# A hybrid retention block on eight cores: the order of the casts in stage A and of the per-head projections

## The chip, the cores and the metric

The kernel runs on the 8 cores of one Trainium2 chip. Each core does the same program on its own two sequences of the batch of 16 (4096 tokens), without talking to the others. The time is device microseconds of the slowest core. Each core has TensorE (PE, with its weight loads PEld), VectorE (DVE), ScalarE (ACT), GpSimd (POOL, unused here) and SyncE (SP, which issues all DMAs of this kernel). Each takes its instructions in the order of its own list.

## The reference

One layer of a streaming encoder, width 1024, 4 retention heads with keys of 256 and values of 512. Cut to what matters here:

```python
h = layer_norm(x, ln0_g, ln0_b)
z = h @ w_in                       # conv (2x1024), q, k (1024), v, g (2048), two gates (1024)
cv, cg, q, k, v, g, ga, gb = split(z)
u = silu(layer_norm(causal_depthwise_conv(cv * sigmoid(cg), conv_w, conv_b)))
y_conv = u @ w_conv_o + b_conv_o
q = rotary(q, positions); k = rotary(k, positions) * dk ** -0.5
# per head, in chunks of 64: intra-chunk scores with decay, plus a carried state
y = ((q @ k.T) * decay) @ v + (q * xi) @ state
state = state * gamma_chunk + (k * zeta).T @ v
r = head_group_norm(y, ret_gn_g)
y_ret = (silu(g) * r) @ w_ret_o
mix = sigmoid(ga + b0) * y_conv + sigmoid(gb + b1) * y_ret
h = layer_norm(alpha * h + mix @ w_out)
# then a gated FFN of 2816 with a causal conv of width 3, a gated per-layer embedding, a last layer_norm
```

## The kernel before

A prologue turns all weights from float32 into bf16 copies in HBM, through FA, HT32 and HID. Then eight blocks of 512 tokens run one after the other (the loop over blk, L476), four for each sequence. A small scheduler (Sched, L46) keeps one list per engine in the order of the Python code; it adds semaphore waits from the records (Buf) that each operation reads and writes, and reorders nothing. So the order of the code is each engine's order of work. All compute instructions are recorded in helpers: matmuls L333, transposes L336, activations L344, tensor_tensor L347, scalar_tensor_tensor L356, copies and casts L359, DMA L362.

Stage A (L483 to L516) takes four tiles (tti) of 128 tokens: XS is loaded (two buffers; the first two tiles of a block are loaded during the block before), DVE takes statistics of XS (L490 to L492, into SMALL), ACT takes the square root, DVE reciprocal and a scalar op (L494, L495), ACT normalises XS in place, PE transposes it in eight pieces into two PSUM banks, ACT writes the eight pieces to HT32 (float32, L508), and DVE casts each to BB (bf16, L510). BB, also called HB, is the moving or stationary operand of all projections.

Then come the positions and the cosine and sine tables CS, the convolution branch, and stage C, the loop over four heads (L607 to L691). For each head h: q and k (16 matmuls of 512 columns each, then six DVE operations of rotary each over RT, into QT and KT_), v (64 matmuls of 256 columns; ACT copies to VV), g (64 more; ACT applies Silu into FC), transposes of KT_ into the bf16 bank PSB and ACT copies with a scale to KZ. Then the retention loop over four tiles of 128 tokens: scores (2 matmuls, one bank), SD = scores x mask on DVE, a product SD x VV and two QT x SBF (one bank, py), two KZ x VV (two banks), from which DVE updates the state SF and ACT its bf16 copy SBF; g1, g2 and g3 normalise py over its row (bn_stats on DVE, square root on ACT, reciprocal and scalar op on DVE, RN on ACT, the product with FC into RB_ on DVE), g2 one tile late and g3 two. At its end 16 transposes of RB_ through PSB and four ACT copies fill RTT. Then the next head begins. QT, KT_, KZ, VV, SD and RB_ have one buffer each, all cut from HID, which the convolution and the FFN also use. alias_barrier carries waits over from one use of HID to the next.

PSUM has seven float32 banks, handed out in a ring by next_ps (L321), and PSB. Weights come through wload (L446): chunks of 512 KB into a ring of four slots WR, issued by SP in the order of the code, each as soon as the matmuls of four chunks earlier are through with the slot.

Of the kernel before, what the change touches and what calls it, by code (L numbers as in the profile page):

```python
# [18 lines left out]
H = 4  # L19
# [241 lines left out]
def build_nc(nblk=NBLK, stop=None):  # L261
# [17 lines left out]
    with contextlib.ExitStack() as st:  # L279
# [33 lines left out]
        PT = sb("PT", [128, 2, TB], BF16)  # L313
        ZHT = sb("ZHT", [128, 176], F32)
# [73 lines left out]
        QT = HID[:, 0:1024].rearrange("p (d t) -> p d t", d=2)  # L388
        KT_ = HID[:, 1024:2048].rearrange("p (d t) -> p d t", d=2)
        KZ = HID[:, 2048:3072].rearrange("p (t d) -> p t d", t=4)  # L390
        VV = HID[:, 3072:5120].rearrange("p (t e) -> p t e", t=4)
        SD = HID[:, 5120:5632].rearrange("p (t i) -> p t i", t=4)
        RB_ = HID[:, 5632:7680].rearrange("p (t e) -> p t e", t=4)
        bQT, bKT, bKZ, bVV, bSD, bRB = Buf("qt"), Buf("kt"), Buf("kz"), Buf("vv"), Buf("sd"), Buf("rb")
        HIDV = HID[:, :].rearrange("p (j t) -> p j t", j=NJ)
        bHID = [Buf("hid%d" % j) for j in range(NJ)]
        hid_groups = {"u": bU, "head": [bQT, bKT, bKZ, bVV, bSD, bRB], "hid": bHID}
# [78 lines left out]
        for blk in range(nblk):  # L476
# [4 lines left out]
            if stop == 'pos':  # L481
                break
            for tti in range(4):  # L483
# [12 lines left out]
                act(XS[:, s, :], XS[:, s, :], AF.Identity, [bXS[s], bsm], [bXS[s]], bias=SMALL[:, c0 + 15:c0 + 16], scale=SMALL[:, c0 + 14:c0 + 15])  # L496
                if stop == 'A1':
                    continue
                for half in range(2):
                    pt_, bpt = next_ps()  # L500
                    for q in range(4):
                        f = half * 4 + q
                        tr(pt_[:, q * 128:(q + 1) * 128], XS[:, s, f * 128:(f + 1) * 128], IDF[:], [bXS[s], bID], [bpt])
                    if stop == 'A2':
                        continue
                    for q in range(4):
                        f = half * 4 + q
                        act(HT32[:, f, tti * 128:(tti + 1) * 128], pt_[:, q * 128:(q + 1) * 128], AF.Identity,  # L508
                            [bpt, bPAR], [bHT[f]], bias=pc("ln0_b", f), scale=pc("ln0_g", f))
                        cp(BB[:, f, tti * 128:(tti + 1) * 128], HT32[:, f, tti * 128:(tti + 1) * 128], [bHT[f]], [bBB[f]])  # L510
# [96 lines left out]
            for h in range(H):  # L607
# [14 lines left out]
                for part in range(2):  # L622
                    Ws = [wload("w_in", (16 if part == 0 else 24) + 2 * h + c2) for c2 in range(2)]
                    for tti in range(4):
                        pb, bpb = next_ps()
                        for c2 in range(2):
                            W, bW = Ws[c2]
                            for kt in range(8):
                                mm(pb[:, c2 * 256:(c2 + 1) * 256], HB[:, kt, tti * 128:(tti + 1) * 128], W[:, kt, :], kt == 0, kt == 7,
                                   [bW, bHB[kt]], [bpb])  # L630
                        if part == 0:
                            act(VV[:, tti, :], pb[:], AF.Copy, [bpb], [bVV])
                        else:
                            act(FC[:, tti, :], pb[:], AF.Silu, [bpb], [bFC[tti]])
# [4 lines left out]
                for tti in range(4):  # L639
                    act(KZ[:, tti, :], PSB[:, tti * 256:(tti + 1) * 256], AF.Copy, [bPSB, bPAR], [bKZ], scale=pc("zs", h))  # L640
                pys = {}

                def g1(tti):
                    c0 = 64 + tti * 16
                    bsm = bSMR[tti]
                    py, bpy = pys[tti]
                    S.op("dve", (lambda p_, c_: lambda e: e.bn_stats(out=SMALL[:, c_:c_ + 6], in_=p_[:]))(py, c0), [bpy], [bsm])  # L647
                    S.op("dve", (lambda c_: lambda e: e.bn_aggr(out=SMALL[:, c_ + 6:c_ + 8], in_=SMALL[:, c_:c_ + 6]))(c0), [bsm], [bsm])
                    act(SMALL[:, c0 + 8:c0 + 9], SMALL[:, c0 + 7:c0 + 8], AF.Sqrt, [bsm, bPAR], [bsm], bias=pc("epsx", h))

                def g2(tti):
                    c0 = 64 + tti * 16
                    bsm = bSMR[tti]
                    py, bpy = pys[tti]
                    rn = tti % 2
                    S.op("dve", (lambda c_: lambda e: e.reciprocal(out=SMALL[:, c_ + 8:c_ + 9], in_=SMALL[:, c_ + 8:c_ + 9]))(c0), [bsm], [bsm])
                    stt(SMALL[:, c0 + 9:c0 + 10], SMALL[:, c0 + 6:c0 + 7], -1.0, SMALL[:, c0 + 8:c0 + 9], ALU.mult, ALU.mult, [bsm], [bsm])
                    act(RN[:, rn, :], py[:], AF.Identity, [bpy, bsm], [bRN[rn]], bias=SMALL[:, c0 + 9:c0 + 10], scale=SMALL[:, c0 + 8:c0 + 9])
# [29 lines left out]
                for e4 in range(4):  # L688
                    for tti in range(4):
                        tr(PSB[:, tti * 128:(tti + 1) * 128], RB_[:, tti, e4 * 128:(e4 + 1) * 128], IDB[:], [bRB, bID], [bPSB])  # L690
                    act(RTT[:, h * 4 + e4, :], PSB[:, 0:512], AF.Copy, [bPSB], [bRTT[h * 4 + e4]])  # L691
            for mp in range(4):
# [174 lines left out]
```

How the kernel before makes its waits and increments, by code:

```python
                def body(eng):  # L139
                    for i, o in enumerate(self.ops[engname]):
                        for (key, val, kind) in o["waits"]:
                            if kind == "c":
                                eng.wait_ge(sems[key][val % NS], cum[key][val])
                            else:
                                eng.wait_ge(sems[key], val)
                        if o["fn"] is None:
                            continue
                        ins = o["fn"](eng)
                        if o["inc"] is not None:
                            ins.then_inc(sems[o["inc"][0]], o["inc"][1])
                        elif o["need"]:
                            ins.then_inc(sems[engname][i % NS], 1)
```

## Time and profile before

| | us |
|---|---|
| median of two runs | 6075.39 |
| the two runs | 6067.71, 6083.07 |
| the profiled execution | 6061.24 |
| its span (slowest core, core 5) | 6059.5 |
| spans of the eight cores | 6040.0 to 6059.5 |
| PE busy | 3906.8 (64%) |
| DVE busy | 2753.4 (45%) |
| ACT busy | 2093.0 (35%) |

The profile is of one execution on the slowest core. Busy times are sums over the span; matmuls are pipelined and their ends are modelled. A row of the timeline gives start, length, engine, line, operation, tiles and count, and in brackets how long the engine was idle before it and which engine, tile and line it then waited for. The granted clock of TensorE is given as a share of full speed (2.4 GHz); here its rows are at 0.50 (1.2 GHz), at 1.00, or at a mean between. Where an instruction waits for several semaphores, the wait is put down to the one that came last.

### The profile page before, as it was taken

The page shows a single profiled execution, that of the slowest core. Times are in us where ns is not written, and L with a number is a line of the kernel's source. Part 1 is how long each engine was busy: PE and PEld are TensorE (multiplying, and loading weights), DVE is VectorE, ACT ScalarE, POOL GpSimd, SP SyncE. Part 2 cuts the span into 40 slices and gives each one's busy share as a digit, 9 for nine tenths or more (in the row PEclk, how much of TensorE's full clock was granted, in tenths as well). Part 3 has the DMA queues.
Part 4 walks back from the last instruction along what each step waited for, and adds up shares of the span by engine and source line. Part 5 has one row for each costly group of instructions (what it writes and reads, how often), then busy time and mean ns, then how long its engine had stood idle before and what let it go on. Part 6 is the DMA issues. An engine that isn't in the chain of part 4 may idle for free.

```text
span 6059.5 us, 61462 instructions; the slowest of 8 cores (6040.0 to 6059.5 us)
## 1 busy us (share of the span) xinstructions
PE 3906.8 (64%) x18688; PEld 1883.6 (31%) x18688; DVE 2753.4 (45%) x4886; ACT 2093.0 (35%) x3448; POOL 0.2 (0%) x4
## 2 busy tenths in 40 slices
PE   0006677586775768667765867767675867757686
PEld 0002332233332333224322343233332333323332
DVE  1214437353464436453374435553374433644354
ACT  1113334323333333333343333333343333433333
POOL 0000000000000000000000000000000000000000
PEclk9999779797897879887787878978797877978798
DMA  9992223221232113212222112222132222321132
GB/s 317 330 321 77 70 73 100 81 68 59 84 108 79 56 56 111 80 58 84 84 85 98 59 57 94 91 72 70 63 107 74 69 69 77 104 83 53 60 107 85
DMA packets 162226, 586.57 MB, mean 97 GB/s; under 512 B 17648, under 2 KB 26480, under 8 KB 151408
## 3 DMA queue, kind: packets, MB, share of 16 engines
q1 hardware_dynamic: 161904, 582.64, 29.0%
q8 instruction: 158, 2.59, 0.2%
q14 instruction: 164, 1.34, 0.1%
HBM read 516.51 MB, written 66.06 MB: 96 GB/s over the span
## 4 chain that ended last, share of the span: by engine, by line
PE 47%; DVE 25%; DMA 9%; ACT 9%; issue 8%; DVEq 1%; SPq 0%; ACTq 0%
PE PS L333 45%; DVE FA L356 10%; DVE HID L347 3%; DVE HT L347 2%; DVE SF L356 2%; DMA WR<-w_ffn_down_bf 2%; ACT HT L344 2%; ACT HID L344 1%; DMA HT<-w_in 1%; DVE FA L347 1%; DVE SMALL L647 1%; ACT RN L344 1%; PE PSB L336 1%; DMA FA<-w_in 1%; ACT RTT L344 1%
## 5 line engine op out<-in xcount | busy, mean ns | idle before, releaser
L333 PE MATMUL PS<-BA,WR 128*128 128x512 bf16 x4352 | 1066.4, 391 | 376.7 <-DVE BA L359 137.4
L333 PE MATMUL PS<-BB,WR 128*128 128x512 bf16 x3072 | 786.9, 415 | 66.6 <-DMA WR<-w_in_bf 56.7
L333 PEld LDWEIGHTS PS<-BA,WR 128*128 128x128 bf16 x4352 | 416.0, 99 | 1005.2 <-issue 575.8
L356 DVE SCALAR_TENSOR_TENSOR FA<-PS,PAR,FA 128x511 f32<-128x511 f32 x704 | 525.5, 746 | 59.8 <-ACT FA L344 21.7
L336 PE MATMUL PS<-IDF,XS 128*128 128x128 f32 x256 | 62.1, 424 | 713.4 <-ACT XS L344 713.4
L344 ACT ACTIVATE FA<-PS,PAR 128x512 f32<-128x512 f32 x416 | 316.6, 761 | 512.5 <-PE PS L333 443.3
L333 PE MATMUL PS<-HID,DG 128*128 128x512 bf16 x1984 | 448.8, 390 | 43.5 <-DVE DG L574 43.5
L333 PEld LDWEIGHTS PS<-BB,WR 128*128 128x128 bf16 x3072 | 322.6, 106 | 491.5 <-issue 191.3
L333 PE MATMUL PS<-HID 128*128 128x512 bf16 (+1 forms) x640 | 224.9, 435 | 372.2 <-ACT RN L344 211.9
L333 PE MATMUL PS<-WR,BB 128*128 128x256 bf16 x4096 | 452.4, 273 | 0.0
L333 PEld LDWEIGHTS PS<-WR,BB 128*128 128x128 bf16 x4096 | 400.8, 98 | 53.2
L333 PE MATMUL PS<-HID,WR 128*128 128x512 bf16 x1408 | 340.1, 401 | 94.2 <-DMA WR<-w_ffn_down_bf 94.2
L574 DVE TENSOR_TENSOR DG<-IDB,PAR 128x3968 bf16<-128x3968 bf16 x64 | 273.9, 4290 | 139.5 <-PE PS L333 139.5
L356 DVE SCALAR_TENSOR_TENSOR SF<-SF,PS 128x512 f32<-128x512 f32 x256 | 164.6, 684 | 290.1 <-PE PS L333 290.0
L333 PEld LDWEIGHTS PS<-HID,DG 128*128 128x128 bf16 x1984 | 196.3, 99 | 296.1 <-issue 72.0
L347 DVE TENSOR_TENSOR RT<-PS,CS 128x512 f32<-128x512 f32 x256 | 168.0, 688 | 263.2 <-PE PS L333 252.9
L347 DVE TENSOR_TENSOR FC<-PS,FC 128x512 f32<-128x512 f32 x128 | 88.5, 692 | 435.3 <-PE PS L333 308.2
L344 ACT ACTIVATE SBF<-SF 128x512 bf16<-128x512 f32 x256 | 157.0, 629 | 357.7 <-DVE SF L356 356.6
L336 PEld LDWEIGHTS PS<-IDF,XS 128*128 128x128 f32 x256 | 50.2, 224 | 723.8 <-issue 723.8
L344 ACT ACTIVATE FC<-PS,PAR 128x512 f32<-128x512 f32 x192 | 131.0, 682 | 398.8 <-PE PS L333 398.6
L344 ACT ACTIVATE BB<-HT 128x512 bf16<-128x512 f32 x128 | 80.6, 629 | 537.6 <-DVE HT L347 460.1
L344 ACT ACT_TABLE_LOAD x145 | 186.0, 1283 | 221.5 <-DVE RT L356 75.4
(91 smaller groups left out, 4073.2 us busy)
## 6 DMA issues: line engine op xcount, KB each, us to landing
WR<-w_in_bf SPq DMA_DIRECT2D x320, 512.0 KB, 3.8
WR<-w_ffn_up_bf SPq DMA_DIRECT2D x176, 512.0 KB, 3.3
WR<-w_ffn_down_bf SPq DMA_DIRECT2D x128, 352.0 KB, 3.2
WR<-w_ret_o_bf SPq DMA_DIRECT2D x64, 512.0 KB, 3.9
FA<-w_in SPq DMA_DIRECT2D x20, 1024.0 KB, 12.2
HT<-w_in SPq DMA_DIRECT2D x20, 1024.0 KB, 12.0
w_in_bf<-HID SPq DMA_DIRECT2D x40, 512.0 KB, 9.1
XS<-x SPq DMA_DIRECT2D x32, 512.0 KB, 3.5
```

Of the source, the lines that this page charges most:

```text
L333: S.op("pe", lambda e: e.matmul(out, lhsT=lhsT, rhs=rhs, start=start, stop=stop), r, w)
L336: S.op("pe", lambda e: e.transpose(out, in_, ident), r, w)
L344: S.op("act", lambda e: e.activation(out=out, in_=in_, func=func, **kw), r, w)
L347: S.op("dve", lambda e: e.tensor_tensor(out=out, in0=in0, in1=in1, op=op), r, w)
L356: S.op("dve", lambda e: e.scalar_tensor_tensor(out=out, in0=in0, scalar=scalar, in1=in1, op0=op0, op1=op1), r, w)
L574: S.op("dve", (lambda g_, f_: lambda e: e.tensor_tensor(out=DG[:, g_, :, :], in0=IDB[:].unsqueeze(1).broadcast_to([128, 31, 128]), in1=PAR ...
L647: S.op("dve", (lambda p_, c_: lambda e: e.bn_stats(out=SMALL[:, c_:c_ + 6], in_=p_[:]))(py, c0), [bpy], [bsm])
```

## The change

Two edits.

Stage A: the eight casts of HT32 to BB are not recorded at once but collected, and recorded after the XS activation of the next tile; those of the fourth tile follow the loop.

Stage C: the body of the head loop is cut into three functions, proj_qkv (q, k, rotary, v), proj_g_kz (g, the transposes of k, KZ) and ret_loop (the rest, unchanged but for the buffers it reads). QT, KT_ and VV get two buffers each, chosen by h % 2; SD moves to a tensor of its own (1 KB per partition). The order becomes qkv(0), g_kz(0), qkv(1), ret(0), g_kz(1), qkv(2), ret(1), g_kz(2), qkv(3), ret(2), g_kz(3), ret(3). The order of the weight chunks on SP and of the PSUM banks follows it.

```diff
+        SDT = sb("SDT", [128, 4, 128], BF16)
...
-        QT = HID[:, 0:1024].rearrange("p (d t) -> p d t", d=2)
-        KT_ = HID[:, 1024:2048].rearrange("p (d t) -> p d t", d=2)
-        KZ = HID[:, 2048:3072].rearrange("p (t d) -> p t d", t=4)
-        VV = HID[:, 3072:5120].rearrange("p (t e) -> p t e", t=4)
-        SD = HID[:, 5120:5632].rearrange("p (t i) -> p t i", t=4)
-        RB_ = HID[:, 5632:7680].rearrange("p (t e) -> p t e", t=4)
-        bQT, bKT, bKZ, bVV, bSD, bRB = Buf("qt"), Buf("kt"), Buf("kz"), Buf("vv"), Buf("sd"), Buf("rb")
+        QTs = [HID[:, 1024 * i:1024 * (i + 1)].rearrange("p (d t) -> p d t", d=2) for i in range(2)]
+        KTs = [HID[:, 2048 + 1024 * i:2048 + 1024 * (i + 1)].rearrange("p (d t) -> p d t", d=2) for i in range(2)]
+        KZ = HID[:, 4096:5120].rearrange("p (t d) -> p t d", t=4)
+        VVs = [HID[:, 5120 + 2048 * i:5120 + 2048 * (i + 1)].rearrange("p (t e) -> p t e", t=4) for i in range(2)]
+        RB_ = HID[:, 9216:11264].rearrange("p (t e) -> p t e", t=4)
+        SD = SDT
+        bQTs, bKTs, bVVs = [Buf("qt0"), Buf("qt1")], [Buf("kt0"), Buf("kt1")], [Buf("vv0"), Buf("vv1")]
+        bKZ, bSD, bRB = Buf("kz"), Buf("sd"), Buf("rb")
         HIDV = HID[:, :].rearrange("p (j t) -> p j t", j=NJ)
         bHID = [Buf("hid%d" % j) for j in range(NJ)]
-        hid_groups = {"u": bU, "head": [bQT, bKT, bKZ, bVV, bSD, bRB], "hid": bHID}
+        hid_groups = {"u": bU, "head": bQTs + bKTs + bVVs + [bKZ, bRB], "hid": bHID}
...
+            deferred_cp = []
            for tti in range(4):
...
                 act(XS[:, s, :], XS[:, s, :], AF.Identity, [bXS[s], bsm], [bXS[s]], bias=SMALL[:, c0 + 15:c0 + 16], scale=SMALL[:, c0 + 14:c0 + 15])
+                for fn_ in deferred_cp:
+                    fn_()
+                deferred_cp = []
...
-                        cp(BB[:, f, tti * 128:(tti + 1) * 128], HT32[:, f, tti * 128:(tti + 1) * 128], [bHT[f]], [bBB[f]])
+                        deferred_cp.append((lambda f_, t_: lambda: cp(BB[:, f_, t_ * 128:(t_ + 1) * 128], HT32[:, f_, t_ * 128:(t_ + 1) * 128], [bHT[f_]], [bBB[f_]]))(f, tti))
+            for fn_ in deferred_cp:
+                fn_()
...
-            for h in range(H):
+            def proj_qkv(h):
+                par = h % 2
+                QT, KT_, VV = QTs[par], KTs[par], VVs[par]
+                bQT, bKT, bVV = bQTs[par], bKTs[par], bVVs[par]
                 for which, (dst, bdst, cbase) in enumerate(((QT, bQT, 8 + h), (KT_, bKT, 12 + h))):
                     W, bW = wload("w_in", cbase)
...
-                for part in range(2):
-                    Ws = [wload("w_in", (16 if part == 0 else 24) + 2 * h + c2) for c2 in range(2)]
-                    for tti in range(4):
-                        pb, bpb = next_ps()
-                        for c2 in range(2):
-                            W, bW = Ws[c2]
-                            for kt in range(8):
-                                mm(pb[:, c2 * 256:(c2 + 1) * 256], HB[:, kt, tti * 128:(tti + 1) * 128], W[:, kt, :], kt == 0, kt == 7,
-                                   [bW, bHB[kt]], [bpb])
-                        if part == 0:
-                            act(VV[:, tti, :], pb[:], AF.Copy, [bpb], [bVV])
-                        else:
-                            act(FC[:, tti, :], pb[:], AF.Silu, [bpb], [bFC[tti]])
+                Ws = [wload("w_in", 16 + 2 * h + c2) for c2 in range(2)]
+                for tti in range(4):
+                    pb, bpb = next_ps()
+                    for c2 in range(2):
+                        W, bW = Ws[c2]
+                        for kt in range(8):
+                            mm(pb[:, c2 * 256:(c2 + 1) * 256], HB[:, kt, tti * 128:(tti + 1) * 128], W[:, kt, :], kt == 0, kt == 7,
+                               [bW, bHB[kt]], [bpb])
+                    act(VV[:, tti, :], pb[:], AF.Copy, [bpb], [bVV])
+
+            def proj_g_kz(h):
+                par = h % 2
+                KT_, bKT = KTs[par], bKTs[par]
+                Ws = [wload("w_in", 24 + 2 * h + c2) for c2 in range(2)]
+                for tti in range(4):
+                    pb, bpb = next_ps()
+                    for c2 in range(2):
+                        W, bW = Ws[c2]
+                        for kt in range(8):
+                            mm(pb[:, c2 * 256:(c2 + 1) * 256], HB[:, kt, tti * 128:(tti + 1) * 128], W[:, kt, :], kt == 0, kt == 7,
+                               [bW, bHB[kt]], [bpb])
+                    act(FC[:, tti, :], pb[:], AF.Silu, [bpb], [bFC[tti]])
                 for tti in range(4):
                     for d in range(2):
                         tr(PSB[:, (tti * 2 + d) * 128:(tti * 2 + d + 1) * 128], KT_[:, d, tti * 128:(tti + 1) * 128], IDB[:],
                            [bKT, bID], [bPSB])
                 for tti in range(4):
                     act(KZ[:, tti, :], PSB[:, tti * 256:(tti + 1) * 256], AF.Copy, [bPSB, bPAR], [bKZ], scale=pc("zs", h))
+
+            def ret_loop(h):
+                par = h % 2
+                QT, KT_, VV = QTs[par], KTs[par], VVs[par]
+                bQT, bKT, bVV = bQTs[par], bKTs[par], bVVs[par]
                 pys = {}
...
+            proj_qkv(0)
+            proj_g_kz(0)
+            for h in range(H):
+                if h + 1 < H:
+                    proj_qkv(h + 1)
+                ret_loop(h)
+                if h + 1 < H:
+                    proj_g_kz(h + 1)
             for mp in range(4):
```

The other lines of the diff rename c0 to c0_ in g1 and g2 and change nothing.

## Rows read from the trace of the kernel before

**Rows 1.** The head of the page.

```profile
span 6059.5 us, 61462 instructions; the slowest of 8 cores (6040.0 to 6059.5 us)
```

**Rows 2.** The page's chain that ended last, shares by engine.

```profile
PE 47%; DVE 25%; DMA 9%; ACT 9%; issue 8%; DVEq 1%; SPq 0%; ACTq 0%
```

**Rows 3.** Waits over the span: total us, times, longest us.

```profile
PE PS L336 <- ACT XS L344: 713.4, 32, 469.3
...
PE PS L333 <- ACT RN L344: 211.9, 64, 3.6
...
PE PSB L336 <- DVE HID L347: 167.4, 32, 5.5
...
PE PS L333 <- ACT HID L344: 29.4, 32, 0.9
```

**Rows 4.** Windows of one head: length, PE, PEld, DVE, ACT, POOL, clock, DMA share, GB/s.

```profile
1407.30:1411.50 4.20, 4.20 (x13) 1.54 (x12) 0.41 (x1) 0.60 (x1) 0.00 (x0) 0.50 0.00 0
1411.50:1430.20 18.70, 18.70 (x151) 14.60 (x150) 7.62 (x12) 5.36 (x8) 0.00 (x0) 1.00 0.31 113
...
1433.30:1436.70 3.40, 0.70 (x4) 0.32 (x4) 2.29 (x5) 1.42 (x3) 0.00 (x0) 0.81 0.17 69
1436.70:1457.20 20.50, 7.62 (x19) 2.11 (x19) 10.43 (x26) 9.05 (x15) 0.00 (x0) 0.50 0.00 1
```

**Rows 5.** Timeline of stage A, block 1, tile 0 to tile 1.

```profile
1174.50 4.11 ACT L344 ACTIVATE HT<-PS,PAR 128x128 f32<-128x128 f32 x8 [1.49 <-PE PS L336]
...
1178.86 0.69 DVE L490 BATCH_NORM_STATS2 SMALL<-XS 128x6 f32<-128x512 f32 x1
1179.65 0.69 DVE L491 BATCH_NORM_STATS2 SMALL<-XS 128x6 f32<-128x512 f32 x1
...
1180.75 0.29 ACT L344 ACTIVATE SMALL<-SMALL,PAR 128x1 f32<-128x1 f32 x1 [2.13 <-DVE SMALL L492]
...
1181.67 1.24 ACT L344 ACTIVATE XS<-XS,SMALL 128x1024 f32<-128x1024 f32 x1 [0.63 <-DVE SMALL L356]
```

**Rows 6.** The same place in block 2, ACT alone.

```profile
1874.27 4.11 ACT L344 ACTIVATE HT<-PS,PAR 128x128 f32<-128x128 f32 x8 [1.49 <-PE PS L336]
...
1881.43 1.24 ACT L344 ACTIVATE XS<-XS,SMALL 128x1024 f32<-128x1024 f32 x1 [0.63 <-DVE SMALL L356]
1884.11 4.11 ACT L344 ACTIVATE HT<-PS,PAR 128x128 f32<-128x128 f32 x8 [1.44 <-PE PS L336]
```

**Rows 7.** Transposes of tile 1, and the XS loads' time to landing.

```profile
1183.16 1.94 PE L336 MATMUL PS<-IDF,XS 128*128 128x128 f32 x8 [7.96 <-ACT XS L344]
...
DMA to landing us min/median/max: 3.3/3.5/6.7
```

**Rows 8.** The end of stage A, block 1: last transposes, first matmuls.

```profile
1203.12 1.94 PE L336 MATMUL PS<-IDF,XS 128*128 128x128 f32 x8 [7.90 <-ACT XS L344]
...
1212.47 14.44 PE L333 MATMUL PS<-BB,WR 128*128 128x512 bf16 x56 [7.40 <-DMA WR<-w_in_bf]
```

**Rows 9.** Timeline at the start of one retention loop.

```profile
1430.29 0.61 PE L336 MATMUL PSB<-IDB,HID 128*128 128x128 bf16 x8
1430.60 0.60 ACT L344 ACTIVATE FC<-PS 128x512 f32<-128x512 f32 x1 [1.15 <-PE PS L333]
...
1430.73 0.28 PE L333 MATMUL PS<-HID 128*128 128x128 bf16 x2
...
1433.41 0.70 PE L333 MATMUL PS<-HID 128*128 128x512 bf16 x4 [0.94 <-ACT HID L344]
```

**Rows 10.** The matmuls of v and g, and the last rotary operation.

```profile
1416.32 14.14 PE L333 MATMUL PS<-WR,BB 128*128 128x256 bf16 x128
...
1420.50 0.69 DVE L347 TENSOR_TENSOR HID<-RT 128x512 bf16<-128x512 f32 x1
```

**Rows 11.** Landing of the two WR loads issued about 1430, and a prologue load.

```profile
DMA to landing us min/median/max: 3.3/3.9/4.4
...
FA<-w_in SPq DMA_DIRECT2D x20, 1024.0 KB, 12.2
```

More of the change, by code:

```diff
@@ L640, in build_nc @@
                     act(KZ[:, tti, :], PSB[:, tti * 256:(tti + 1) * 256], AF.Copy, [bPSB, bPAR], [bKZ], scale=pc("zs", h))
+            def ret_loop(h):
+                par = h % 2
+                QT, KT_, VV = QTs[par], KTs[par], VVs[par]
+                bQT, bKT, bVV = bQTs[par], bKTs[par], bVVs[par]
                 pys = {}
                 def g1(tti):
-                    c0 = 64 + tti * 16
+                    c0_ = 64 + tti * 16
                     bsm = bSMR[tti]
                     py, bpy = pys[tti]
-                    S.op("dve", (lambda p_, c_: lambda e: e.bn_stats(out=SMALL[:, c_:c_ + 6], in_=p_[:]))(py, c0), [bpy], [bsm])
-                    S.op("dve", (lambda c_: lambda e: e.bn_aggr(out=SMALL[:, c_ + 6:c_ + 8], in_=SMALL[:, c_:c_ + 6]))(c0), [bsm], [bsm])
-                    act(SMALL[:, c0 + 8:c0 + 9], SMALL[:, c0 + 7:c0 + 8], AF.Sqrt, [bsm, bPAR], [bsm], bias=pc("epsx", h))
+                    S.op("dve", (lambda p_, c_: lambda e: e.bn_stats(out=SMALL[:, c_:c_ + 6], in_=p_[:]))(py, c0_), [bpy], [bsm])
+                    S.op("dve", (lambda c_: lambda e: e.bn_aggr(out=SMALL[:, c_ + 6:c_ + 8], in_=SMALL[:, c_:c_ + 6]))(c0_), [bsm], [bsm])
+                    act(SMALL[:, c0_ + 8:c0_ + 9], SMALL[:, c0_ + 7:c0_ + 8], AF.Sqrt, [bsm, bPAR], [bsm], bias=pc("epsx", h))
                 def g2(tti):
-                    c0 = 64 + tti * 16
+                    c0_ = 64 + tti * 16
                     bsm = bSMR[tti]
@@ L655, in g2 @@
                     rn = tti % 2
-                    S.op("dve", (lambda c_: lambda e: e.reciprocal(out=SMALL[:, c_ + 8:c_ + 9], in_=SMALL[:, c_ + 8:c_ + 9]))(c0), [bsm], [bsm])
-                    stt(SMALL[:, c0 + 9:c0 + 10], SMALL[:, c0 + 6:c0 + 7], -1.0, SMALL[:, c0 + 8:c0 + 9], ALU.mult, ALU.mult, [bsm], [bsm])
-                    act(RN[:, rn, :], py[:], AF.Identity, [bpy, bsm], [bRN[rn]], bias=SMALL[:, c0 + 9:c0 + 10], scale=SMALL[:, c0 + 8:c0 + 9])
+                    S.op("dve", (lambda c_: lambda e: e.reciprocal(out=SMALL[:, c_ + 8:c_ + 9], in_=SMALL[:, c_ + 8:c_ + 9]))(c0_), [bsm], [bsm])
+                    stt(SMALL[:, c0_ + 9:c0_ + 10], SMALL[:, c0_ + 6:c0_ + 7], -1.0, SMALL[:, c0_ + 8:c0_ + 9], ALU.mult, ALU.mult, [bsm], [bsm])
+                    act(RN[:, rn, :], py[:], AF.Identity, [bpy, bsm], [bRN[rn]], bias=SMALL[:, c0_ + 9:c0_ + 10], scale=SMALL[:, c0_ + 8:c0_ + 9])
                 def g3(tti):
```

## The prediction

> **What bounds the kernel now.** I read the page's head and its chain first, then the waits, then windows over one head, then the timeline of the two places that the diff touches. The span is 6059.5 us and nothing repeats but the eight blocks, about 699 us each ((6059.5 - 469.3) / 8) behind a prologue of 469.3 us, which is PE's longest wait [rows 1, 3]. In the chain no engine holds all of it: PE has 47%, DVE 25%, ACT 9% [rows 2]. So the kernel is a string of stages with different limits, and a change is worth what the last wait of its own stage is worth. The waits of PE name those of our two stages [rows 3]: 713.4 us for the normalised input tile XS (469.3 of them the prologue, so 244.1 us over 32 tiles, 7.6 us each), 211.9 us for RN inside the retention loop, 167.4 us for the product RB ahead of the closing transposes, 29.4 us for KZ (0.92 us in each of the 32 heads). The windows of one head show its shape [rows 4]: 22.9 us of dense projections (1407.3 to 1430.2), then a retention loop in which PE is busy 0.70 + 7.62 us of 23.9 us, so that 15.6 us are idle. The granted clock falls to its lower level, 0.50, in that loop, and the next projections start with 4.2 us at 0.50 before they run at 1.00.
>
> **Part 1, the casts to BB put off by one tile.** On DVE the statistics of tile t+1 now stand behind the eight casts of tile t, and each cast waits for its HT activation. So after the last HT activation of tile 0 ends (1174.50 + 4.11 = 1178.61) the chain is two bn_stats, bn_aggr, the square root on ACT at 1180.75, reciprocal and scalar op, and the XS activation at 1181.67: a gap of 3.06 us [rows 5]. Block 2 has 3.05 us (1878.38 to 1881.43) [rows 6]. With the casts behind, the statistics are done while ACT is still busy with HT; the square root follows the last HT activation after some 0.05 us, and the rest of the chain is what it was, 1181.67 - 1180.75 = 0.92 us. The gap becomes 0.97, a gain of 2.09 us. The order on ACT is unchanged, so the eight HT activations still stand ahead of the square root, and no more is to be had. It happens between the tiles of a block, 3 times in each of 8: 24 x 2.09 = 50.2 us.
>
> Covers: (a) the put-off casts go at some 0.3 us each (estimate from statistics that start 0.8 us apart for a 0.69 us duration [rows 5], applied to a short cast) and finish 2.7 us behind the scalar op; the HT activations that overwrite their sources start 2.68 us after the XS activation and go on for 4.1 us (1881.43 to 1884.11) [rows 6], so cast f is done before activation f comes. (b) The reload of XS for tile t+2 starts when the transposes of tile t end, 3.4 us after its XS activation starts (1181.67 [rows 5] to 1183.16 + 1.94), and lands in 3.5 us, 6.7 at worst [rows 7]. At a new period of 7.8 us its statistics are wanted by 14.5 us and can be done by 3.4 + 6.7 + 1.8 = 11.9 us even with the worst landing. (c) The casts of the fourth tile run as before. (d) Behind the stage SP issues the next block's XS, the positions and the first weights, all after the last transposes; the first matmul starts 7.4 us behind them, on the weights [rows 8]. It moves with them, so the 6.3 us per block pass on. Bounds: 1.7 us per tile if half of what I put down to the statistics' cover is eaten by queueing, 2.3 if all of the 3.06 but the 0.8 us of square root, reciprocal and scalar op goes: 41 to 55 us.
>
> **Part 2, the head loop turned.** PE's order per head was q k v g KZ, retention; it becomes g KZ of this head, q k v of the next, retention. Nothing is put between the instructions of the retention loop. PE takes them in order, and so the 15.6 us idle in it stay, as do the waits for RN and RB [rows 3, 4]. What the Trainium skill says (TensorE: Matmul & The Clock Gate, Step-by-step: what each phase is for) speaks against a larger gain too: matmuls stay in program order, only weight loads are pulled ahead. By that rule the overlap named in the code would be worth nothing inside the loop; the trace agrees so far that matmuls behind the loop never start before its end.
>
> What does change is the start of the loop. Today the KZ transposes run at 1430.29, the first scores at 1430.73, and the KZ matmuls wait 0.94 us for ACT to 1433.41 [rows 9]. With q k v of the next head in between, KZ is some 14 us old (6.9 + 7.1, below): the wait goes for heads 0, 1 and 2, and stays for head 3, which has no successor. 24 x 0.92 = 22.1 us. What could be late next is behind ACT and DVE. On ACT the copy of the next head's last V tile stands directly ahead of the loop. The loop doesn't read it (its own head's V lies in the other buffer), and its 0.60 us start some 0.3 us after the last matmul, as the last Silu's do today (1430.29 to 1430.60 [rows 9]), well ahead of the first SBF activation. On DVE the next head's rotary stands ahead, which is costed below. So I take the whole 22.1 us. Bounds: 0 (another wait takes its place) and 22.1.
>
> Other moves, costed at nothing: DVE now gets the rotary of head h+1 ahead of the SD product of head h. Today the rotary of K ends at 1421.2, 4.9 us after the V matmuls began [rows 10], and those of V take 7.1 us (half of the 14.14), so 2.2 us are spare. The first score, the first SD x V product and the first KZ product take PSUM banks that this rotary reads, so without the spare time each us over it would be a us of PE at 24 places. The weights: g, q, k of the coming burst now load during retention; the pair for V is issued at the end of g and is wanted after KZ (0.6 us) and the 32 matmuls of q and k, 7.5 us later (those take 1407.3 to 1416.3 today, 4.2 us of it at half the clock, so 9.0 - 2.1 = 6.9 us at the full one [rows 4, 10]). The same pair, issued at the same point today, lands in 3.3 to 4.4 us [rows 11]. The slow 4.2 us at a burst's start now fall on g (256 columns) instead of q; the burst still has one such start per head, and head 3 has its own (a short burst of g alone), so four per block as before. PSUM: each head still takes 28 banks of the ring of seven, and each bank's predecessor is read by then. RB transposes and RTT copies are not touched.
>
> **Sum.** 50.2 + 22.1 = 72.3 us off the profiled execution: 6059.5 - 72.3 = 5987.2 us of span. That execution took 6061.24 us, 14.2 us (0.23%) under the median of the two runs shown, 6075.39. Off the median: 6075.4 - 72.3 = 6003.1 us, -1.2%. Two per cent is about what a measurement of this kernel can tell from no change.
>
> **Rivals.**
> A. The head part gives nothing or a little loss, because the loop's first step is held by something else (ACT's or DVE's new queue order): only part 1 stays, 6075 - 50 = 6025 us. For it: the waits are small beside the loop. Against: KZ is the releaser in all 32 heads [rows 3].
> B. The projections do fill the loop's holes: 15.6 us x 24 = 374 us, so 6075 - 50 - 374 = 5651 us. For it: the idle time is there. Against: the emitted order.
> C. The other side: the V weights come late. Their cover shrinks from the whole loop (over 23 us) to 7.5 us. Two chunks of 512 KB are the bytes of one prologue load, which took 12.2 us under load [rows 11]; at that rate PE waits 4.7 us in 24 places, +113 us: 6075 - 72 + 113 = 6116 us. It turns the change slower once the landing passes 7.5 + 72/24 = 10.5 us, and by 2% once it passes 7.5 + 8.0 = 15.5 us. Against: 4.4 us as the longest in the row of the same pair.
> D. The change doesn't do what it says in stage A: the statistics are held by something other than the casts (the reload of XS), so only the head's 22 us stay: 6053 us. Against: the statistics of tile 1 start 0.25 us after the last HT activation ends [rows 5], and tiles 0 and 1 are loaded before the block begins.
>
> **How the numbers follow.** Forecast 0.75, A 0.12, B 0.03, C 0.04, D 0.06. The forecast's own bounds are 41 to 55 us and 0 to 22 us, so 41 to 77 us of gain, 5998 to 6034 us. The shown runs scatter by 8 us about their median and the profiled one lies 14 us under it, which widens this to 5980 to 6042. A lies inside; B, C and D lie outside with 0.13, and I leave some more for the widths. Faster by over 2% (under 5954 us) is B, with 0.01 for a gain that I don't see: 0.04. Slower by over 2% is the far part of C: 0.02. Within 2% is the rest, 0.94.
>
> **What would show it.** Gap from the last HT activation to the next XS activation: 1.0 us instead of 3.05. PE's wait for XS down by some 50 us to 663. PE's wait for KZ at 8 places instead of 32, 7.4 us. PE's waits for RN and RB as they are (212 and 167 us), the loop's windows as idle as now. A new wait of PE for w_in weights ahead of v, or of the first SD for DVE, would break part 2; statistics that wait for XS from DMA would break part 1; PE busy over 40% between first score and RB transposes would prove B.

## The result and the profile after

The ratio of the changed kernel's time to the kernel before is 0.9853, with a 95% interval of 0.9832 to 0.9873. On the 6075.39 us of before that is 5986 us, 89 us less (77 to 102). The profiled execution took 5983.27 us against 6061.24 us, 78 us less. The plain medians over all executions are 6291.49 us (11 of the changed kernel) and 6354.41 us (10 of the kernel before). In seven executions of either kernel one die or both ran at a lower granted clock, and the ratio and all that follows compare executions, or dies, without that.

The head of the page of the changed kernel and its chain by engine, which answer to [rows 1, 2]:

```profile
span 5981.5 us, 61614 instructions; the slowest of 8 cores (5961.9 to 5981.5 us)
...
PE 48%; DVE 25%; DMA 10%; ACT 8%; issue 8%; DVEq 1%; SPq 0%; ACTq 0%
```

The chain has the same shape, with PE and DMA one point up and ACT one point down. The waits of PE in the changed kernel (total us, times, longest us), which answer to [rows 3]; its lines stand one lower, L334 for matmuls and L337 for transposes:

```profile
PE PS L337 <- DVE SMALL L494: 468.4, 1, 468.4
...
PE PS L334 <- ACT RN L345: 212.4, 64, 3.7
PE PS L337 <- ACT XS L345: 195.8, 31, 8.0
PE PSB L337 <- DVE HID L348: 168.4, 32, 5.5
...
PE PS L334 <- DVE SDT L348: 129.8, 128, 2.9
...
PE PS L334 <- DMA WR<-w_in_bf: 57.9, 7, 12.1
...
PE PS L334 <- ACT HID L345: 8.4, 8, 1.1
```

The wait for XS, prologue included, is 468.4 + 195.8 = 664.2 us instead of 713.4. The wait for KZ (ACT HID) is left in 8 places with 8.4 us, where it had 32 with 29.4. The waits for RN and RB are what they were, 212.4 and 168.4 us. No wait for w_in weights has been added (57.9 us in 7 places; before, 56.7 us in 7).

Stage A in block 1, ACT alone (start, length, engine, line, operation, tiles, and in brackets the idle time before and its releaser), which answers to [rows 5, 6]:

```profile
1161.44 1.24 ACT L345 ACTIVATE XS<-XS,SMALL 128x1024 f32<-128x1024 f32 x1 [0.63 <-DVE SMALL L357]
1164.16 4.11 ACT L345 ACTIVATE HT<-PS,PAR 128x128 f32<-128x128 f32 x8 [1.49 <-PE PS L337]
1168.17 0.28 ACT L345 ACTIVATE SMALL<-SMALL,PAR 128x1 f32<-128x1 f32 x1
1169.08 1.24 ACT L345 ACTIVATE XS<-XS,SMALL 128x1024 f32<-128x1024 f32 x1 [0.63 <-DVE SMALL L357]
1171.97 4.45 ACT L345 ACTIVATE HT<-PS,PAR 128x128 f32<-128x128 f32 x8 [1.65 <-PE PS L337]
1176.32 0.28 ACT L345 ACTIVATE SMALL<-SMALL,PAR 128x1 f32<-128x1 f32 x1
1177.22 1.24 ACT L345 ACTIVATE XS<-XS,SMALL 128x1024 f32<-128x1024 f32 x1 [0.62 <-DVE SMALL L357]
```

The square root at 1168.17 stands directly behind the last HT activation, and the XS activation follows at 1169.08, 0.81 us after 1164.16 + 4.11. From one XS activation to the next it is 7.64, 8.14 and 7.98 us in this block, where it was 9.90, 10.12 and 9.84. But the eight HT activations of tile 1 take 4.45 us, those of tile 0 4.11.

The start of one retention loop, PE alone, which answers to [rows 9]:

```profile
1411.42 0.61 PE L337 MATMUL PSB<-IDB,HID 128*128 128x128 bf16 x8
...
1425.76 0.28 PE L334 MATMUL PS<-HID 128*128 128x128 bf16 x2
1426.58 0.38 PE L334 MATMUL PS<-HID,SDT 128*128 128x512 bf16 x1 [0.55 <-DVE SDT L348]
1426.80 0.59 PE L334 MATMUL PS<-SBF,HID 128*128 128x512 bf16 x2
1427.22 0.70 PE L334 MATMUL PS<-HID 128*128 128x512 bf16 x4
1430.36 0.38 PE L334 MATMUL PS<-HID,SDT 128*128 128x512 bf16 x1 [2.43 <-DVE SDT L348]
...
1435.86 0.37 PE L334 MATMUL PS<-HID 128*128 128x128 bf16 x2 [3.49 <-ACT RN L345]
```

KZ was transposed at 1411.42, 14 us ahead of the loop, and the two KZ products, the first two of the four matmuls at 1427.22, wait for nothing (the other two are the scores of tile 1). The rest is as before: the scores of tile 2 at 1435.86 still wait 3.49 us for RN, with PE idle.

Where the 78 us went, in us, from the start times of the matmuls in both traces, summed over the eight blocks and averaged over the eight cores, from the first XS transpose to the start of the last matmul:

| part | before | after | difference |
|---|---|---|---|
| stage A, first to last XS transpose | 250.2 | 201.5 | -48.7 |
| from there to the first matmul | 58.5 | 60.3 | +1.8 |
| convolution branch | 1140.7 | 1136.9 | -3.8 |
| q, k, v, g and KZ transposes | 733.0 | 732.0 | -1.0 |
| retention loops (first score to first RB transpose), heads 0 to 2 | 630.6 | 600.7 | -29.9 |
| retention loops, head 3 | 209.9 | 210.4 | +0.5 |
| RB transposes | 148.7 | 149.0 | +0.3 |
| all behind the heads | 2401.9 | 2405.5 | +3.6 |
| sum | 5573.5 | 5496.3 | -77.2 |

Two parts carry it: stage A with 2.03 us for each of 24 gaps, and the 24 loops that have a successor with 1.25 us each.

### The profile page after: what moved, and what is told of

It reads as the page before. It is cut to its first block, busy times and chain, and to the rows that moved or that the text cites. A ratio compares the mean times of both kernels' runs of the same rounds, so it can differ in the third digit from the quotient of the medians.

```text
span 5981.5 us, 61614 instructions; the slowest of 8 cores (5961.9 to 5981.5 us)
## 1 busy us (share of the span) xinstructions
PE 3896.3 (65%) x18688; PEld 1894.0 (32%) x18688; DVE 2736.0 (46%) x4886; ACT 2092.7 (35%) x3448; POOL 0.2 (0%) x4
## 4 chain that ended last, share of the span: by engine, by line
PE 48%; DVE 25%; DMA 10%; ACT 8%; issue 8%; DVEq 1%; SPq 0%; ACTq 0%
PE PS L334 46%; DVE FA L357 10%; DVE HT L348 2%; DVE HID L348 2%; DVE SF L357 2%; DMA WR<-w_ffn_down_bf 2%; PE PSB L337 1%; DMA HT<-w_in 1%; ACT HT L345 1%; DVE FA L348 1%; DVE SMALL L672 1%; DMA FA<-w_in 1%; ACT RN L345 1%; ACT RTT L345 1%; DVE ST L467 1%
## 5 line engine op out<-in xcount | busy, mean ns | idle before, releaser
L334 PE MATMUL PS<-BA,WR 128*128 128x512 bf16 x4352 | 1066.4, 391 | 376.7 <-DVE BA L360 137.0
L334 PE MATMUL PS<-BB,WR 128*128 128x512 bf16 x3072 | 735.5, 395 | 69.2 <-DMA WR<-w_in_bf 57.9
L334 PEld LDWEIGHTS PS<-BA,WR 128*128 128x128 bf16 x4352 | 416.2, 99 | 1005.2 <-issue 576.0
L334 PE MATMUL PS<-WR,BB 128*128 128x256 bf16 x4096 | 504.5, 289 | 0.0
L337 PE MATMUL PS<-IDF,XS 128*128 128x128 f32 x256 | 62.1, 424 | 664.2 <-DVE SMALL L494 468.4
L334 PE MATMUL PS<-HID,DG 128*128 128x512 bf16 x1984 | 449.5, 390 | 43.3 <-DVE DG L582 43.3
L334 PEld LDWEIGHTS PS<-BB,WR 128*128 128x128 bf16 x3072 | 308.3, 101 | 455.3 <-issue 126.7
L334 PEld LDWEIGHTS PS<-WR,BB 128*128 128x128 bf16 x4096 | 424.5, 104 | 77.3
L334 PE MATMUL PS<-HID,WR 128*128 128x512 bf16 x1408 | 340.0, 401 | 94.3 <-DMA WR<-w_ffn_down_bf 94.3
L348 DVE TENSOR_TENSOR RT<-PS,CS 128x512 f32<-128x512 f32 x256 | 168.0, 688 | 399.8 <-PE PS L334 389.8
L334 PE MATMUL PS<-HID 128*128 128x128 bf16 (+1 forms) x512 | 156.7, 411 | 220.8 <-ACT RN L345 212.4
L334 PEld LDWEIGHTS PS<-HID,DG 128*128 128x128 bf16 x1984 | 196.4, 99 | 296.4 <-issue 72.6
L348 DVE TENSOR_TENSOR FC<-PS,FC 128x512 f32<-128x512 f32 x128 | 88.6, 692 | 435.3 <-PE PS L334 308.8
L337 PEld LDWEIGHTS PS<-IDF,XS 128*128 128x128 f32 x256 | 50.2, 223 | 674.5 <-issue 674.5
```

The source lines that it names most:

```text
L334: S.op("pe", lambda e: e.matmul(out, lhsT=lhsT, rhs=rhs, start=start, stop=stop), r, w)
L337: S.op("pe", lambda e: e.transpose(out, in_, ident), r, w)
L348: S.op("dve", lambda e: e.tensor_tensor(out=out, in0=in0, in1=in1, op=op), r, w)
```

## The experiments

All kernels start from the kernel before or from the changed one, as said. "Total" is the sum of the table above.

**Each part alone.** The first kernel is the kernel before with the casts put off:

```diff
-                        cp(BB[:, f, ...], HT32[:, f, ...], [bHT[f]], [bBB[f]])
+                        deferred_cp.append(...)   # run behind the next XS activation
```

> The kernel before with the first part of the change alone (casts of a tile recorded behind the XS activation of the next). Theory (the two parts add): stage A, first to last XS transpose, goes from 250 us over eight blocks to 202 us, everything else as before: 48 to 49 us less, -0.8%. Rival (the whole gain of some 78 us in the span is this part, the head loop's numbers being a shift of waits): -1.3%.

Measured: the profiled execution 6008.47 us, the three lowest 6008 to 6012 and a fourth 6045.86, against 6059 to 6065 us for the kernel before on that chip. Stage A is 201.4 us, the loops of heads 0 to 2 stay at 628.6, the total is 5520.6, 52.9 us less. The second is the changed kernel with that diff taken back:

> The changed kernel with the casts to BB back in their old place, so the turned head loop alone. Theory: the retention loops of heads 0 to 2 go from 26.3 to 25.0 us, 29 to 30 us less in all, -0.5%; stage A stays at 250 us. Rival (turning the loop gives nothing by itself): within 0.1% of before.

Measured: 6031 to 6042 us in five executions. Stage A 250.0 us, loops of heads 0 to 2 601.9 us (28.7 less), total 5546.7, 26.8 us less. The two totals add up to 79.7 us against 77.2 for both, so the parts add up to within 2.5 us, and two thirds of the gain (52.9 of 79.7) are the casts.

**KZ early, without a second buffer.** In the kernel before, the KZ transposes and copies move from behind g to between v and g:

```diff
                 for part in range(2):
+                    if part == 1:
+                        # the eight KZ transposes and the four KZ copies
                     Ws = [wload("w_in", (16 if part == 0 else 24) + 2 * h + c2) for c2 in range(2)]
```

> The kernel before, heads in the old order and with single buffers, but the KZ transposes and copies stand between v and g instead of behind g. Theory (all that the turned loop gives is the age of KZ at the start of the retention loop): each of the 32 retention loops loses the same 1.25 us, the fourth head's too, about 40 us less, -0.65%, more than the turned loop gives, without a second buffer. Rival (the gain of 1.25 us is 0.92 us of KZ wait and the rest comes from what else the new order moves): 29 us less, -0.5%. Second rival (the KZ copies now stand ahead of the Silus on ACT and hold FC or a PSUM bank up): a new wait of PE in the g matmuls and less than 20 us gained.

The start of a retention loop of this kernel, PE alone:

```profile
1420.12 0.28 PE L333 MATMUL PS<-HID 128*128 128x128 bf16 x2
1421.05 0.38 PE L333 MATMUL PS<-HID 128*128 128x512 bf16 x1 [0.65 <-DVE HID L347]
1421.26 0.59 PE L333 MATMUL PS<-SBF,HID 128*128 128x512 bf16 x2
1421.69 0.71 PE L333 MATMUL PS<-HID 128*128 128x512 bf16 x4
```

The KZ products, the first two of the four matmuls at 1421.69, start 0.43 us after the products with SBF, without a wait. The loops of heads 0 to 2 take 604.2 us (26.4 less) and those of head 3 take 200.9 (9.0 less): 35.4 us, or 1.11 us in each of 32, and no wait of g for the KZ copies appeared. That lies between the 40 us of the theory and the 29 us of the rival: the age of KZ is most of what the turned loop gives (1.11 of 1.25 us per loop). Because it reaches all 32 loops, one block moved by a few lines takes more out of the loops (35.4 us) than the second buffers do (29.9 us in 24). The time says less: 6034 to 6043 us, about 25 us less than before instead of 40, total 5553.5. The difference stands behind the heads (2417.7 us against 2401.9), where the matmuls of the down projection are slower on average. The row of its group (count | busy us, mean ns | idle):

```profile
L333 PE MATMUL PS<-HID,WR 128*128 128x512 bf16 x1408 | 351.9, 411 | 98.5 <-DMA WR<-w_ffn_down_bf 98.5
```

In the kernel before the same group has 340.1 us and a mean of 401 ns. From the granted clock in both traces, the stretch from the embedding's transposes to the first of the last transposes (HT) of a block spends 212 us, over all blocks, at the granted clock of 0.50 here (mean of the cores) and 179 us before; 33 us more at half the speed are some 16 us, an estimate from these two figures. Nothing in that stretch was edited. Why the clock falls there more often here is open; the changed kernel has 189 us there and the put-off casts alone 186.

**The casts in reverse.** The changed kernel with one word more:

```diff
-                for fn_ in deferred_cp:
+                for fn_ in reversed(deferred_cp):
                     fn_()
```

> The changed kernel with the put-off casts of a tile recorded in reverse order, feature 7 first. In the changed kernel each of the eight HT activations of tiles 1 to 3 carries a wait of its own on the cast that reads its target, and the eight take 4.45 us instead of 4.11. Theory (those are the 0.34 us, one more wait instruction of some 0.055 us in each): with the last cast belonging to feature 0, the first activation's wait covers the others, the eight take 4.11 us again, and stage A loses another 24 x 0.34 = 8 us against the changed kernel, a total of -1.4 to -1.6% against before. Rival (the activations really wait for the casts, or both engines slow each other down at the same memory): 4.45 us stay, or a wait shows at the first activation.

ACT in stage A of core 2, tiles 1 to 3 of block 1:

```profile
1168.75 3.56 ACT L345 ACTIVATE HT<-PS,PAR 128x128 f32<-128x128 f32 x7 [0.37 <-ACT HT L345]
...
1173.12 1.24 ACT L345 ACTIVATE XS<-XS,SMALL 128x1024 f32<-128x1024 f32 x1 [0.62 <-DVE SMALL L357]
1175.85 4.11 ACT L345 ACTIVATE HT<-PS,PAR 128x128 f32<-128x128 f32 x8 [1.49 <-PE PS L337]
...
1180.77 1.24 ACT L345 ACTIVATE XS<-XS,SMALL 128x1024 f32<-128x1024 f32 x1 [0.62 <-DVE SMALL L357]
```

The activations take 4.11 us again (the row at 1168.75 is seven of the eight), and from one XS activation to the next it is 7.65 us (1173.12 to 1180.77). Stage A is 196.6 us, 4.9 less than in the changed kernel and not the 8 of the theory: only the activations of tiles 1 and 2 lie between the first and the last XS transposes, and 16 x 0.34 is 5.4 us. The trace of the changed kernel shows a second wait instruction ahead of each of the eight activations (six of them start 0.055 us later for it), where this one has it once: in this scheduler the order in which buffers are given back decides how many waits their writers carry. The same casts run in the same stretch and the eight take 4.11 us again, so the rival, two engines that slow each other down, fell. The profiled execution took 6000.66 us and the lowest 5980.1, against 5980.4 for the changed kernel, so the time shows no gain. The same kernel again:

> The changed kernel with the put-off casts in reverse order again, because its stage A came out 5 us shorter than the changed kernel's while the end of the kernel did not. Theory (the 5 us are real, and the rest is where the slower clock falls in the later stages, which differs from execution to execution): stage A 196 to 197 us again against 201.5, and the time 5975 to 5990 us. Rival (the reversal costs as much later as it gives): stage A 196 us and a time of 5990 us or more.

Stage A is 196.6 us again. The profiled execution took 6021.18 us, outside the 5975 to 5990 of the theory; on that chip the kernel before took 6096.6 us at its lowest. Die 0 has a median span of 5964.7 us and die 1 6013.7, the changed kernel's dies 5975.0 and 5968.0. The 5 us in stage A are shown; that they reach the end is not, since they are no more than the spread between dies, and the rival of this run is not ruled out.

**The bank behind the wait for RN.** In the kernel before, the retention loop takes fixed PSUM banks:

```diff
-                    psc, bpsc = next_ps()
+                    psc, bpsc = PSF[0], bPS[0]
-                    py, bpy = next_ps()
+                    py, bpy = PSF[3 + tti], bPS[3 + tti]
-                        pk, bpk = next_ps()
+                        pk, bpk = PSF[1 + d], bPS[1 + d]
```

> The kernel before with one edit in the retention loop: instead of taking PSUM banks from the ring of seven, the scores always take bank 0, the two state products banks 1 and 2, and py bank 3 + tile. Question: what holds the 3.3 us that PE waits for RN twice in each head, 212 us in all, and which neither double buffers nor the new order touch. Theory (the ring hands the bank of py of tile t to the scores of tile t+2, so the scores wait for RN of tile t although they need nothing of it): the wait for RN goes to zero, the tiles' period falls from 6.5 us to what the state's own chain takes, 4.4 to 5 us, in two or three of four tiles, 3 to 5 us per retention loop, 100 to 160 us in 32, -1.6 to -2.6%. Rival (the loop is paced by the chain of state and statistics on DVE and ACT, and the bank is only the last of several waits): PE's wait moves to SD or SBF and less than 40 us come back.

Measured: 5986 to 5992 us in three executions, a ratio of 0.985 (0.981 to 0.989), as much as the whole change under study. The loops of heads 0 to 2 take 567.4 us (63.2 less), those of head 3 188.4 (21.5 less), q to KZ 721.4 (11.6 less), and 10 us are lost again behind the heads; total 5487.4, 86 us less. In the kernel before the scores of tile 2 wait for RN, and the products with SD of tiles 2 and 3 lie 6.50 us apart:

```profile
1442.36 0.37 PE L333 MATMUL PS<-HID 128*128 128x128 bf16 x2 [3.29 <-ACT RN L344]
1443.28 0.59 PE L333 MATMUL PS<-HID 128*128 128x512 bf16 x1 [0.54 <-DVE HID L347]
...
1449.78 0.59 PE L333 MATMUL PS<-HID 128*128 128x512 bf16 x1 [0.54 <-DVE HID L347]
```

PE in one loop with the fixed banks, products of tiles 1 to 3:

```profile
1430.00 0.58 PE L333 MATMUL PS<-HID 128*128 128x512 bf16 x1 [2.67 <-DVE HID L347]
...
1431.24 1.27 PE L333 MATMUL PS<-HID 128*128 128x512 bf16 x4
1434.95 0.59 PE L333 MATMUL PS<-HID 128*128 128x512 bf16 x1 [2.44 <-DVE HID L347]
...
1436.18 1.27 PE L333 MATMUL PS<-HID 128*128 128x512 bf16 x4
1440.49 0.59 PE L333 MATMUL PS<-HID 128*128 128x512 bf16 x1 [3.04 <-DVE HID L347]
```

From product to product it is now 4.95 and 5.54 us. No wait for RN is left, and the one for SD has grown, from 131.2 us to this:

```profile
PE PS L333 <- DVE HID L347: 278.8, 130, 3.4
```

So the theory holds for its cause and not for its size: 2.6 us per loop instead of 3 to 5, because the next wait in line is the one for SD, whose multiplication stands on DVE behind the statistics of the tile before.

**The loop filled.** The changed kernel, casts reversed, with q, v and k of head h+1 recorded inside the loop of head h, g between the last tile and the RB transposes, and fixed banks in the loop (not shown in this excerpt):

```diff
                     tt(SD[:, tti, :], psc[:, 0:128], MK[:, h, :], ALU.mult, [bpsc, bMK], [bSD])
+                    grp[tti][0]()        # q a, v 0, v 2, k a
                     mm(py[:], SD[:, tti, :], VV[:, tti, :], True, False, [bSD, bVV], [bpy])
...
+                    grp[tti][1]()        # q b, v 1, v 3, k b
                     g1(tti)
...
                 g3(3)
+                proj_g(h + 1)
+                rots[4]()                # rotary of k
                 for e4 in range(4):
```

> The changed kernel (with the casts of stage A in reverse order) with the overlap really written into PE's order: during the four tiles of the retention loop of head h, one projection group of head h+1 stands between the scores and the product with SD, and one behind the state products (q, then v, then k), and the g matmuls stand between the last tile and the RB transposes. Fixed PSUM banks: four for the loop, two for q and k, one for v; the rotary of q stands on DVE in tiles 1 and 2, that of k behind the last product. Theory (PE takes its list in order, so the idle time of the loop can be had only by work recorded inside it): the loop's tiles take 4.6 to 5.5 us and hide the 14 us of q, k and v and the 5.2 us before the RB transposes; per head 52 us become 31 to 36, 24 times 16 to 21 us, so 380 to 500 us less than the changed kernel, -8 to -10% against before; the granted clock no longer falls inside the loops of heads 0 to 2. Rival (DVE, with 5.4 us of work in tiles 1 and 2, becomes the bound and PE waits in order behind it): 200 to 300 us less. Rival (the idle time is latency of a chain that the added work stretches, since each of PE's in-order groups delays the state's products by 1.7 us): under 150 us less.

Measured: a ratio of 0.9126 (0.907 to 0.918), profiled 5547.58 us, total 5049.4, 524 us less than before and 447 less than the changed kernel. These 447 us are not the filling alone: the fixed banks took 84.7 us out of the loops of the kernel before by themselves, and the reversed casts 4.9 us; a filled loop on the ring, or the changed kernel with fixed banks only, was not run. In this kernel the ring hands g the two banks that the rotary of k, recorded behind it, still has to read, so its k of heads 1 to 3 isn't the reference's; the work is the same in kind and number. The next kernel swaps the two:

```diff
-                proj_g(h + 1)
                 rots[4]()
+                proj_g(h + 1)
```

> The same filling of the retention loop's idle time, with the rotary of the next head's k recorded ahead of the g matmuls instead of behind them, so that it reads its two banks before the ring hands them out again. Theory (as for the filled kernel before it, whose 5552 us stand for this edit too, since DVE is free there): 5540 to 5570 us, -8.5 to -9% against before; the loops of heads 0 to 2 take about 29 us with the g matmuls in them, and what stands between two loops shrinks to the KZ transposes, 0.7 us. Rival (the rotary ahead of the g matmuls holds two banks up and PE waits inside g for it): up to 4 us in 24 places, 96 us more.

Here the rival's mechanism came true. The wait of PE for the rotary on core 0, and the end of a loop with the g matmuls:

```profile
PE PS L334 <- DVE RT L348: 57.2, 16, 7.3
...
1317.23 1.89 PE L334 MATMUL PS<-BB,WR 128*128 128x512 bf16 x8
1326.18 9.09 PE L334 MATMUL PS<-WR,BB 128*128 128x256 bf16 x64 [7.05 <-DVE RT L348]
```

PE waits 7.05 us for the rotary here; others of the 16 waits fall inside g, by where the ring stands in that head. The loops with their g take 771.0 us on die 0 (695.2 in the kernel before this one), 76 us more where the rival said 96, and die 0's spans are 5592 to 5617 us (5536 to 5546). The forecast of 5540 to 5570 us missed: the lowest of eleven executions took 5631.32. The rotary is hidden only as long as nobody needs its banks. The last edit gives g other banks:

```diff
-                    pb, bpb = next_ps()
+                    gb = (6, 0, 1, 2)[tti]
+                    pb, bpb = PSF[gb], bPS[gb]
```

> The filled loop with k's rotary ahead of the g matmuls, as in the kernel before it, where PE waited up to 7 us inside g for that rotary because the ring of seven handed g the two banks that it still read. One edit: the four g groups take banks 6, 0, 1, 2. Theory (only the bank held PE up): the wait of PE for RT goes to zero, the loops of heads 0 to 2 with their g matmuls take 27 to 29 us in all blocks, and the time is 5520 to 5555 us, -8.5 to -9% against before. Rival (DVE is the bound behind the last tile, RB and rotary in one queue): the wait moves to the RB transposes, 4 us in 24 places stay, 5600 us and more.

Measured: a ratio of 0.9093 (0.9071 to 0.9115), 5538 to 5557 us in four executions, total 5049.7; the loops of heads 0 to 2 with their g take 676.0 us, 28.2 each, as the theory said. No wait for the rotary (RT L348) is left. PE of core 0 in the same place, tile 1 of a loop and then g:

```profile
1302.24 0.28 PE L334 MATMUL PS<-HID 128*128 128x128 bf16 x2
1302.35 1.91 PE L334 MATMUL PS<-WR,BB 128*128 128x256 bf16 x16
1304.10 0.38 PE L334 MATMUL PS<-HID,SDT 128*128 128x512 bf16 x1
1304.31 0.59 PE L334 MATMUL PS<-SBF,HID 128*128 128x512 bf16 x2
1304.74 0.59 PE L334 MATMUL PS<-HID 128*128 128x512 bf16 x2
1305.17 1.91 PE L334 MATMUL PS<-WR,BB 128*128 128x256 bf16 x16
...
1317.61 7.15 PE L334 MATMUL PS<-WR,BB 128*128 128x256 bf16 x64
```

The scores, the v group, the three products of py, the two of KZ and the next v group follow each other without idle time, and g (7.15 us for 64 matmuls at the full clock) starts when the last group ends. The waits of PE for RB, RN and SD on that core:

```profile
PE PSB L337 <- DVE HID L348: 42.2, 8, 5.5
...
PE PS L334 <- ACT RN L345: 29.4, 19, 1.9
...
PE PS L334 <- DVE SDT L348: 13.6, 17, 0.9
```

RB has 42.2 us in 8 places (head 3, which isn't filled) instead of 168.4 in 32, RN 29.4 us instead of 212.4, SD 13.6 us instead of 129.8 (the second figures are those of the changed kernel's slowest core). The dies' medians:

```profile
die 0 (median of its cores): 5511.0 us, clock 0.879
die 1 (median of its cores): 5545.7 us, clock 0.869
```

This version beats both kernels: about 9% under the one before, and 7.7% under the changed one (0.9093 / 0.9853 = 0.923, from two separate comparisons). The comparison's own verdict is unclear, but die 0 by itself says the same: 5511.0 us against medians of 6044.9 to 6051.6 us in three executions of the kernel before on that chip, 8.9% less, and against 5975.0 of the changed kernel, 7.8% less.

## Why the prediction came out as it did

**The number and the range.** The predicted 6003 us and the range of 5980 to 6042 us hold the executions of the changed kernel that the ratio compares (5980.4 to 5983.3 us) and miss the median over all of them, 6291.49. The step that failed is the base: "Off the median: 6075.4 - 72.3" took the median of two runs, 15 us apart, for the level of both kernels, and the range was widened only by their scatter of 8 us and the 14 us of the profiled one. What the runs showed in its place: the kernel before itself has a median of 6354.41 us over ten executions, seven of them between 6263 and 6532 us, and the changed kernel has seven of eleven between 6063 and 6502 us. Why those are longer stays open. An absolute forecast from so few runs carries a term that no row of the trace gives. The forecast of the difference, -1.2%, lies outside the measured interval too, by 0.1 of a point (-1.27 to -1.68%), and the next two points take up the terms of its sum, 77.2 us measured against 72.3. The 89 us that the ratio gives are 11 more than the two profiled executions show; no row accounts for these.

**Part 1, right in its mechanism, sized within 2 us.** Forecast 24 x 2.09 = 50.2 us, measured 48.7. Two errors nearly cancel. The gap fell from 3.05 to 0.81 us, not to 0.97, because the square root starts as the last activation drains; and the HT activations of tiles 1 and 2 grew by 0.34 us each, since each carries a wait for its own cast. So 24 x 2.24 - 16 x 0.34 = 48.3 us. Cover (a) asked whether the casts would be late. They were not; the wait instructions themselves cost the time. The covers for the reload of XS and for the stages behind held.

**Part 2, right in its mechanism, a quarter too small.** Forecast 24 x 0.92 = 22.1 us, named as an upper bound; measured 29.9, and 28.7 with this part alone. The term mis-sized is the wait for KZ, which I took from the idle time of PE. Idle time is counted from the modelled end of the matmul before. In [rows 9] that is about 0.16 us later than the next matmul of a dense stream would start: the products with SBF and those of KZ stand 0.42 us apart in the changed kernel (1426.80 to 1427.22) although the first two are shown with 0.59 us. So each wait is 0.94 + 0.16 = 1.10 us long, and moving KZ alone gave 1.11. The remaining 0.14 us per loop are partly at the first product with SD (idle 0.55 us instead of 0.66) and partly in tile 1, whose product with SD is shown with 0.38 us instead of 0.58: it starts at 1430.36, and the granted clock falls to 0.50 at 1430.7, where before it fell at 1435.4, ahead of that product at 1436.78. How the 0.14 us divide was not tested.

**What stays idle.** The forecast that nothing recorded outside the loop can fill it was right: RN 212.4 us, RB 168.4, as before. The Trainium skill (TensorE: Matmul & The Clock Gate, Step-by-step: what each phase is for) says that matmuls stay in program order; the traces agree, with an unchanged wait when the projections stood ahead of the loop, and 447 us less, fixed banks included, when they stood in it.

**The rivals.** A (the head part gives nothing) fell with the second kernel, -26.8 us. B (the holes fill by themselves) fell. Filled by hand, and with fixed banks, the kernel gave 447 us, more than its 374. The 374 count a window that leaves out the first 2.6 us of each loop, the fixed banks shorten the loop by themselves, and the clock stays up: from the first matmul of a block to the first matmul on the heads' outputs (RTT) the cores spend 587 us at 0.50 in the filled kernel of ratio 0.9126, and 1164 in the changed one (granted clock in the traces, all blocks). How the 447 us divide among these was not tested. C (late V weights) fell: waits for w_in weights are 57.9 us against 56.7. D (the statistics held by XS) fell, with the gap at 0.81 us. "Costed at nothing" was right for the rotary, the weights and the RB transposes. The cold start of a burst stayed one per head: g takes 9.40 and 8.42 us in two heads, against 7.15 at the full clock:

```profile
1402.18 9.40 PE L334 MATMUL PS<-WR,BB 128*128 128x256 bf16 x64
...
1455.40 8.42 PE L334 MATMUL PS<-WR,BB 128*128 128x256 bf16 x64
```

## What to carry to other kernels

The double buffers bought no overlap on PE, which took its matmuls in the recorded order; the work must be recorded inside the stall it is to fill, and its buffers and banks chosen so that nothing it needs is handed out meanwhile. Before that, ask of each wait whether it is for data or for a buffer's turn: a ring of seven banks cost this kernel as much as the whole change gave. When a price is read from PE's idle time, add the overlap of pipelined matmuls (0.16 us per wait here), and when a release is put off, count the waits that its users then carry.

## What the runs showed of the hardware that I had not expected

One more wait ahead of an ACT activation costs about 0.055 us even when what it waits for is long done (4.45 against 4.11 us for eight activations, of which six start later for it). The granted clock of a stage changed when only the stages ahead of it were edited: from the embedding's transposes to the first of the last ones the time at 0.50 was 179 us before, 189 in the changed kernel and 212 with KZ moved, by the estimate above up to 16 us of time, near the 27 us that the turned loop gives. Each figure is from one execution per kernel, so its scatter is not known.
